# Partial sums of the output projection inside the attention heads of a four-layer hybrid network

## The reference, cut to what matters

```python
for l in range(2):                       # kind A, twice
    proj = rms_norm(x, attn_norm[l]) @ w_in[l]
    out_a = swa_mixer(...)               # 6 heads of 64, window 128
    out_b = pool_mixer(...)              # 256 values
    out_c = mla_mixer(...)               # 6 latent heads of 64
    x = x + concatenate([out_a, out_b, out_c]) @ w_out[l]
    x = x + (silu(h @ w_gate[l]) * (h @ w_up[l])) @ w_down[l]   # h = rms_norm(x, ...)
# then kind R (a recurrence and 4 cross heads of 128) and kind F (8 fox heads of 64, 4 cross heads):
    x = x + concatenate([y_mix, y_mem]) @ w_out_2[layer]
    x = x + square(relu(rms_norm(x) @ w1)) @ w2
```

## Time and profile before

| | us |
|---|---|
| median of three runs | 2550.38 (2547.52 to 2551.61) |
| the profiled execution | 2546.21 |
| its span | 2544.4 |
| PE busy | 2385.7 (94%) |
| POOL busy | 1687.4 (66%) |
| DVE busy | 1128.1 (44%) |
| ACT busy | 490.2 (19%) |

### The profile page before, as it was taken

How to read it: one execution, slowest core, us unless ns; L and a number is a source line. 1 busy time by engine, 2 the same in 40 slices (tenths; PEclk the granted TensorE clock), 3 DMA queues, 4 the chain that set the end, 5 groups by cost and what they waited for, 6 DMA issues and landing times.

```text
span 2544.4 us, 29116 instructions
## 1 busy us (share of the span) xinstructions
PE 2385.7 (94%) x10786; PEld 1918.6 (75%) x10786; DVE 1128.1 (44%) x1322; ACT 490.2 (19%) x910; POOL 1687.4 (66%) x1370
## 2 busy tenths in 40 slices
PE   5988999999997899999998789999999888999999
PEld 4666788888766678888886568888887775888887
DVE  7764543322476444332248645315344443550440
ACT  3245211110124521111010511001111153210000
POOL 5465677777756567776776577767765644776774
PEclk9988999999998899999999899999999989999999
DMA  4210122223220012222332112222232200222222
GB/s 142 84 45 18 67 87 95 99 85 101 105 89 30 18 67 95 89 97 85 102 122 72 50 66 100 99 99 84 97 116 83 84 17 17 85 98 98 99 99 83
DMA packets 37840, 207.88 MB, mean 82 GB/s; under 512 B 3532, under 2 KB 10316, under 8 KB 16888
## 3 DMA queue, kind: packets, MB, share of 16 engines
q1 hardware_dynamic: 37752, 206.70, 23.3%
HBM read 204.55 MB, written 2.13 MB: 81 GB/s over the span
## 4 chain that ended last, share of the span: by engine, by line
PE 57%; DVE 6%; POOL 2%; ACT 2%; issue 1%; DVEq 0%; POOLq 0%; ACTq 0%
PE ps L822 17%; PE ps L826 17%; PE ps L827 17%; POOL wl L650 1%; PE ps L1183 1%; PE ps L895 1%; PE ps L1157 1%; DVE nt L1707 1%; DVE uc L1707 1%; DVE nt L1699 1%; ACT rt L1333 1%; DVE t L1707 0%; POOL wh L644 0%; POOL act L722 0%; ACT nt L1333 0%
## 5 line engine op out<-in xcount | busy, mean ns | idle before, releaser
L650 POOL TENSOR_TENSOR wl<-raw,wh 128x512 fp32r<-128x512 f32 (+1 forms) x776 | 1051.1, 1385 | 0.0
L644 POOL TENSOR_SCALAR wh<-raw 128x1024 fp32r<-128x1024 f32 (+1 forms) x388 | 431.1, 1131 | 614.9 <-PE ps L822 480.4
L822 PE MATMUL ps<-h,wh 128*128 128x512 f32 x1576 | 619.2, 393 | 28.1 <-POOL wl L650 9.4
L826 PE MATMUL ps<-h,wh 128*128 128x512 f32 x1576 | 615.0, 390 | 0.0
L827 PE MATMUL ps<-h,wl 128*128 128x512 f32 x1576 | 615.0, 390 | 0.0
L822 PE MATMUL ps<-act,wh 128*128 128x512 f32 x1120 | 437.8, 391 | 3.0 <-POOL act L722 1.9
L826 PE MATMUL ps<-act,wh 128*128 128x512 f32 x1120 | 436.6, 390 | 0.0
L827 PE MATMUL ps<-act,wl 128*128 128x512 f32 x1120 | 436.4, 390 | 0.0
L822 PEld LDWEIGHTS ps<-h,wh 128*128 128x128 f32 x1576 | 296.9, 188 | 100.2 <-issue 29.5
L826 PEld LDWEIGHTS ps<-h,wh 128*128 128x128 f32 x1576 | 297.0, 188 | 62.3 <-issue 1.0
L827 PEld LDWEIGHTS ps<-h,wl 128*128 128x128 f32 x1576 | 296.8, 188 | 62.2
(11 more groups left out here) (339 smaller groups left out, 2838.1 us busy)
## 6 DMA issues: line engine op xcount, KB each, us to landing
raw<-w_gu SPq DMA_DIRECT2D x44, 1024.0 KB, 4.8
raw<-w_up SPq DMA_DIRECT2D x32, 1024.0 KB, 4.8
raw<-w_down_b SPq DMA_DIRECT2D x32, 1024.0 KB, 4.9
raw<-w_down_a SPq DMA_DIRECT2D x32, 704.0 KB, 4.0
raw<-w_in_a SPq DMA_DIRECT2D x14, 1024.0 KB, 4.9
raw<-w_in_f SPq DMA_DIRECT2D x13, 1024.0 KB, 4.9
raw<-w_in_r SPq DMA_DIRECT2D x11, 1024.0 KB, 4.9
raw<-w_out_a SPq DMA_DIRECT2D x8, 1024.0 KB, 7.7
```

The lines of the kernel that those rows point to most:

```text
L644: pool.tensor_scalar(hi_s[:, part], raw[s][:, part], 1.0, 1.0, ALU.mult, ALU.mult).then_inc(hi_done, 1)
L650: ins = pool.tensor_tensor(lo_s[:, part], raw[s][:, part], hi_s[:, part].bitcast(F32), ALU.subtract)
L822: first = pe.matmul(out, w_hi, v_hi, start=start, stop=False)
L826: pe.matmul(out, w_hi, v_lo, start=False, stop=False)
```

## The change

In the latent heads of kind A and in the cross heads of kind F, PE computes the part of the projection whose inputs exist already, as sums of their own: slices 0 to 4 in kind A (window heads and pooling; 15 matmuls a tile), slices 0 to 3 in kind F (fox heads; 12 matmuls a tile). A table says which tiles follow in which step; DVE adds each to x (`residual`). After the last head `out_rest` computes the other slices of each tile (9 matmuls in kind A, 12 in kind F), which `resid` adds as before. The weights' blocks are ordered to suit, in the same four chunks. Kind A uses bank 5 for it, kind F banks 6 and 7. POOL splits the second weight chunk of kind A in step 5 of the window heads, the third and fourth in steps 5 and 6 of the latent heads, and the two pooled tiles in step 1 of the latent heads; in kind F the third chunk in step 4 of the cross heads. The first partial sum of each mixer waits until all eight `mixed` parts before it are split. Kind R keeps `out_proj`.

```diff
+MLA = Mixer("causal", "mla", 6, 1, 96, MLA_SCALE, 5, 32, 6,
+            Partials(5, (5,), {2: ((0,), ()), 3: ((1,), (2,)), 4: ((3,), (4,)), 5: ((5,), (6,)), 6: ((7,), ())}))
+XA_F = Mixer("full", "xa", 4, 1, 128, XA_SCALE, 4, 32, 0,
+             Partials(4, (6, 7), {2: ((0,), (1,)), 3: ((2,), (3,)), 4: ((4, 5, 6, 7), ())}))
 # POOL
-                    if m.name == "mla" and hd == m.heads:
+                    if m.name == "mla" and hd == 1:
+                        pool.wait_ge(ready[3], bk.filled(3, -1))
                         for j in range(2):
                             mixed(slice(0, P), 3 + j, up[:, j, :])
-                    attention(SWA, MLA, 3)
-                    attention(MLA, second_at=3, slot_done=7)
+                    attention(SWA, MLA, {3: None, 5: (7, 2)})
+                    attention(MLA, None, {5: None, 6: None})
-                    attention(XA)
-                split_all(n_out - 2, nblk)
+                    attention(XA_F, None, {4: None})
+                    split_all(1, nblk)
 # PE, in attention()
                     if m.starts(hd):
                         prep(m, m.starts(hd))
+                    for d in m.partials.at(hd, 0):
+                        partial(m, d)
                     if hd < m.heads:
                         score_columns(hd)
...
                     if hd + 1 < m.heads:
                         score_rows(hd + 1, 1)
+                    for d in m.partials.at(hd, 1):
+                        partial(m, d)
+            def partial(m, d):
+                b, u = m.partial_use(d)
+                kt = m.partials.k_tiles
+                if d == 0:
+                    pe.wait_ge(mixed_ready, mixr.up(8))
+                pe.wait_ge(free[b], bk.emptied(b, u - 1))
+                for k in range(kt):
+                    last = out_block(d * kt + k, b, k, k == 0, k == kt - 1)
+                last.then_inc(ready[b], 1)
+            def out_rest(k0, waits):
+                def block(d, k):
+                    return out_block(KT * k0 + d * (KT - k0) + k - k0, d % 2, k, k == k0, k == KT - 1)
+                for c in range(KT // 2):
+                    for j in range(2):
+                        pe.wait_ge(free[j], bk.emptied(j, -1))
+                        for k in range(k0, KT - 1 if c == 0 else KT):
+                            if c == 0 and j == 0:
+                                pe.wait_ge(mixed_ready, mixr.up(waits))
+                            last = block(2 * c + j, k)
+                        if c:
+                            last.then_inc(ready[j], 1)
+                    if c == 0:
+                        pe.wait_ge(mixed_ready, mixr.up(waits))
+                        for j in range(2):
+                            block(j, KT - 1).then_inc(ready[j], 1)
+                    bk.close({0: 1, 1: 1})
-                    out_proj([6, 0, 0, 6, 0, 0, 0, 2])
+                    out_rest(5, 2)
 # DVE, in attention()
+                def residual(d):
+                    b, u = m.partial_use(d)
+                    dve.wait_ge(ready[b], bk.filled(b, u))
+                    tt(x[:, d, :], x[:, d, :], ps[b][:, :], ALU.add, bk.empties(b, u))
                     if hd >= 2:
                         out(hd - 2)
+                    for d in m.partials.at(hd, 0):
+                        residual(d)
...
                         maxima(hd + 1, 1)
+                    for d in m.partials.at(hd, 1):
+                        residual(d)
```

More of the change, by code:

```diff
@@ L196, in late, with __init__, at @@
     return {b: n for b, n in uses.items() if b < 6}
+class Partials:
+    def __init__(self, k_tiles, banks, places):
+        self.k_tiles, self.banks, self.places = k_tiles, banks, places
+    def at(self, hd, late):
+        return self.places.get(hd, ((), ()))[late]
 class Mixer:
-    def __init__(self, kind, name, heads, per_unit, rows, scale, tile0, group, kidx):
+    def __init__(self, kind, name, heads, per_unit, rows, scale, tile0, group, kidx, early=None):
         self.kind, self.name, self.heads, self.per_unit = kind, name, heads, per_unit
+        self.partials = early or Partials(0, (), {})
         self.rows, self.scale, self.tile0, self.group, self.kidx = rows, scale, tile0, group, kidx
@@ L251, in uses, with partial_use @@
             uses[5] = h
+        return uses
+    def partial_use(self, d):
+        banks = self.partials.banks
+        b = banks[d % len(banks)]
+        return b, self.own_uses().get(b, 0) + d // len(banks)
+    def uses(self):
+        uses = self.own_uses()
+        for b in self.partials.banks:
+            uses[b] = uses.get(b, 0) + KT // len(self.partials.banks)
         return uses
@@ L632, in split @@
                 if slot_done is not None:
-                    pool.wait_ge(ready[slot_done], bk.filled(slot_done, -1))
+                    pool.wait_ge(ready[slot_done[0]], bk.filled(*slot_done))
                 elif not first:
@@ L1231, in _, with out_block @@
             bias_loaded = [0]
+            out_slot = [0]
+            def out_block(n, b, k, start, stop):
+                if n % BLOCKS == 0:
+                    out_slot[0] = chunk()
+                s, j = out_slot[0], n % BLOCKS
+                return passes(ps[b][:, :], wh[s][:, j, :], wl[s][:, j, :], act[:, k, 0, :], act[:, k, 1, :], start, stop)
+            def partial(m, d):
[24 more added lines that the diff above has]
+                    bk.close({0: 1, 1: 1})
             def out_proj(waits):
@@ L1302, in _ @@
                         in_r()
-                        v = rxv
+                        attention(XA, lambda hd, j: rxv[:, j, hd * P:(hd + 1) * P], 2)
+                        out_proj([1, 1, 2, 2, 0, 0, 1, 1])
                     else:
@@ L1647, in _ @@
                         in_f()
-                        attention(FOX, l, XA)
-                    attention(XA, l)
+                        attention(FOX, l, XA_F)
+                    attention(XA if kind == "R" else XA_F, l)
                 row_squares(norm_after(l, "mixer"))
@@ L2353, in in_a_weights, with early_rows @@
                    blocks(u), k_nope, v_mla, pad, blocks(qb), pairs_of_blocks(v["pool_w"][l])])
+def early_rows(w, k0):
+    b = blocks(w).reshape(P, KT, KT, P)
+    return [b[:, :, 0:k0].reshape(P, -1, P), b[:, :, k0:].reshape(P, -1, P)]
 def mem_weights(w):
@@ L2386 @@
         "w_in_a": np.stack([in_a_weights(v, l) for l in range(2)]),
-        "w_out_a": np.stack([chunks([blocks(w_out[l])]) for l in range(2)]),
+        "w_out_a": np.stack([chunks(early_rows(w_out[l], MLA.partials.k_tiles)) for l in range(2)]),
         "w_gu": np.stack([chunks([blocks(gate_up[l])]) for l in range(2)]),
@@ L2395 @@
                          + mem_weights(v["w_mem_kv_2"][1])),
-        "w_out_b": np.stack([chunks([blocks(v["w_out_2"][l])]) for l in range(2)]),
+        "w_out_b": np.stack([chunks([blocks(v["w_out_2"][0])]),
+                             chunks(early_rows(v["w_out_2"][1], XA_F.partials.k_tiles))]),
         "w_up": np.stack([np.stack([chunks([blocks(w1[l][:, s * half:(s + 1) * half])]) for s in range(2)])
```

29 lines of the change are left out of this document (13 added, 16 removed).

## The result

The changed kernel takes 2598.59 us in the median (2594.63 to 2600.09, 4 runs), the kernel before 2549.77 (2547.52 to 2551.61) beside it: ratio 1.019, 95% interval 1.0178 to 1.0203. It is slower by 49 us. The profiled execution took 2600.09 us, span 2598.0. First the page's busy times, which answer to the earlier trace rows.

The account below looks back on a forecast made before the run. The prediction took PE, busy 94% of the span, as the bound. Layers 0, 1 and F add 21.3 + 16.9 + 11.9 = +50 us, giving 2600 from the median of 2550.4; range 2570 to 2616.

Parts of the forecast that it names:

- Moved matmuls: Matmuls moved before the last head's end lengthen PE's path there: +27.5 us per kind A layer, +22.0 in layer F.
- Gaps filled: Tail of kind A's latent heads: waits of 1.49 and 3.70 us and 1.75 us of slow clock go, -6.9 us.
- The new wait: First partial sum in kind A waits 3.9 us for POOL's pooled tiles, plus 1.7 of slow clock: +5.6 us.
- First addition: First addition to x after the last product: 10.1 us in layer 0, 5.7 in layer 1, 5.8 in F.
- Seven steps: Seven tiles after the first addition, DVE setting the pace: 27.5 us against 33.84 in kind A, 29.3 in F.
- The lead pair: After the eighth addition: PE stands 5 us idle, then starts the lead pair at 1.2 GHz, +1.9 us.
- Sum: Whole kernel: layers 0, 1 and F add 21.3, 16.9 and 11.9 us, layer R nothing; +50 in all.
- Rival B: Cheap loss: pooled-tile wait costs nothing, clock stays up, all DVE steps 3.59 us; +24, 2574 us; chance 20%.
- rival C: Behind the heads DVE keeps its old pace, 33.84 us for seven additions; 2617 us; chance 12%.
- rival A: Heads hide the moved matmuls in PE's gaps: 2523 us if all vanish, even at 65% hidden; chance 5%.

Follow-up runs that it names:

- e5: Changed kernel with each partial sum multiplying slice 0 only, 264 matmuls left out: 2547.81 us, ratio 0.9998.
- e4: Kernel before with only POOL's order changed (pooled tiles in step 0 of latent heads, second weight chunk in step 5 of window heads), no partial sums: 2541.62 us.
- e9: e8 with layer 0's decay rates moved behind the gated tiles of its feed-forward: 2532.18 us, ratio 0.994.
- e1: Changed kernel with POOL splitting the two pooled tiles in step 0 of the latent heads instead of step 1: 2585.12 us, ratio 1.0145.
- e2: Changed kernel with DVE adding tile k to x before it normalizes tile k-1, behind the mixers only: 2563.62 us, ratio 1.0067.
- e6: Changed kernel with layer 0's decay rates moved behind the gated tiles of its feed-forward: 2592.32 us, ratio 1.0169.
- e11: Kernel before with only layer 0's decay rates moved behind the gated tiles: 2548.89 us, ratio 1.000.
- e3: Kernel before with DVE adding tile k to x before it normalizes tile k-1: 2548.52 us, ratio 1.000.
- e8: Changed kernel with e1 and e2, but a partial sum for tile 2 only, directly before the last head's product: 2538.76 us, ratio 0.9958.
- e7: Changed kernel with the edits of e1, e2 and e6 together: 2552.17 us, ratio 1.0013.
- e10: e9 without additions ahead, each tile of x normalized before the next is added: 2540.21 us, ratio 0.9962.

## Why the prediction was right

Forecast 2600, measured 2598.6, and the mechanism was the forecast's, with some single terms off. By its own steps, sizes from the trace of after:

- *Moved matmuls, +27.5 and +22.0.* In layer 0 the point behind the last product came 30.8 later (258.99 to 289.83), 25.7 without the marker; in layer 1 25.3 (893.88 to 945.38, less the 26.2 before it). Forecast 26.2 for both. e5 shows by removal that this term is real.
- *Gaps filled, -6.9.* Right in size: no wait and 2.32 us. But the prediction lays both gaps to POOL, and that holds for less than half: e4 took POOL's part away and gained 3.1 us, which left a wait of 2.12 us and all of the slow clock behind it. With a partial sum in that place as well (e9) both are gone.
- *The new wait, +5.6.* 3.96 us idle against 3.9. The nine matmuls after it start 0.43 us apart instead of 0.23 (232.67 to 236.68), 1.96 us against 1.7; in layer 1 it is 1.6. e1 confirms the pair. The matmuls are at 1.2 GHz there and at 2.4 before and afterwards; the Trainium skill ("TensorE: Matmul & The Clock Gate", section "Why this matters for your kernels") warns of just such gaps between bursts, and the trace agrees.
- *First addition.* 10.1 after the product in layer 0 (289.83 to 299.96), as forecast; in layer 1 5.7 (945.38 to 951.11), as forecast. In kind F it came 15.9 us later than before (2157.10 to 2214.51, less 41.5), forecast 14.5; the 1.4 us too many are the fox product's clock, and with that product at 2.42 it is 13.9 and 12.7 in the traces of e1 and e2. e6 and e11 together show that the decay rates came out of hiding.
- *Seven steps, 27.5.* 27.62 and 27.35; in kind F 28.36 against a forecast of 29.3. The sum was right, its parts less so: in layer 0 two steps were stretched, to 5.11 and 4.60, and five were 3.58, where the forecast had three of at most 4.65 and four of 3.6. The prediction also misreads its row of 3.59 us (278.87 to 282.46): that is a step that falls into POOL's pause between two splits, 279.99 to 281.95 in the trace before, and the steps beside POOL are those of 4.66. The forecast used both numbers as if it had read them so. e2 and e3 show that DVE's order holds the pace, and that it did not before.
- *The lead pair, +1.9.* The wait was 5.06, 5.38 and 4.35 us against "about 5". From the eighth addition on the stages were longer by 2.0, 2.5 and 1.6 us (in layer 0, 26.17 less 24.18).
- *Sum.* Layers 0, 1 and F: 21.0, 16.5 and 12.1 against 21.3, 16.9 and 11.9. Layer R, forecast 0, gave 1.2 back without a change. That layer F hits its forecast within 0.2 us is luck in part: 1.7 of its 12.1 us are the fox product's clock, which was not forecast and which the change didn't cause.

Rival B (a cheap loss) failed on the wait of 3.96 us and the slow matmuls, rival C on the steps of 3.58, and rival A on e5. The Trainium skill's remark on interleaving regimes ("Perfetto Trace Analysis", section "Optimization Strategy") holds where the regime that receives the work has idle time on the engine that bounds the kernel: not for the eight partial sums of the changed kernel (45.00 of 45.00 busy, +49 us), but for the one of e8 and e9, put into an idle stretch of PE.

## What to carry to other kernels

Moving work of the busiest engine is worth the idle time of that engine at the place that receives it, and no more: here 15 matmuls before one product paid, 120 did not. Price also what the moved work had hidden where it came from, since it comes onto the path at once: here thirty tiny operations, and a round trip between two engines in the loop behind, which a reordering of two statements took out. When a stage changes hands from one engine to another, edits that were worth nothing before have to be tried again.

## What the runs showed of the hardware

- Traces of one program differ by some 5 us in their first 225 us. e8 and e9 are the same up to 253 us, and their markers are 224.53 and 220.08; the granted clock from 200 to 230 us was 0.67 in the one and 0.81 in the other. Two single traces are compared only after that is taken off.
- The same product after the same wait ran at either clock level. The fox product of layer F waits 1.46 or 1.47 us in every trace; its eight matmuls take 2.42 us in before, e1, e2, e4 and e7 to e10, and 4.11 in the changed kernel, e3, e5, e6 and e11. A wait of 2.33 us before the lead pair left TensorE at full clock (e2), one of 2.12 before the last product did not (e4). What decides these runs don't settle.
- Operations of DVE on 128 x 4 elements take 0.16 to 0.17 us alone and 0.99 to 1.20 us beside POOL's split (e8), those with one tensor input too. Additions of two on-chip tensors of 128 x 512 take 0.69 alone and 1.33 beside it (305.61 us in the changed kernel's trace). The Trainium skill ("GPSIMD Engine Reference", section "1. Specifications") says that GpSimd contends with DVE instructions that have two on-chip inputs or are in a 2-port mode; for the large additions the trace agrees, and in which mode the small operations with one input ran no run here shows.
